# Projecting the raw residual and applying the norm's root to the output, at three stage borders of a two-model float32 kernel

## What is computed

```python
def rms_norm(x, g):
    xf = x.astype(jnp.float32)
    y = xf * lax.rsqrt(jnp.mean(xf * xf, axis=-1, keepdims=True) + EPS)
    return (y * g.astype(jnp.float32)).astype(x.dtype)
...
        u = rms_norm(h, norm_mix_pre[l])
        proj = u @ w_in[l]
...
        x = x + hybrid_mixer(rmsnorm(x, norm_mix_w[l]), w_in[l], ...)
...
        x = x + peer_ffn(rmsnorm(x, norm_ffn_w[l]), peer_wq[l], peer_subkeys[l], peer_u[l], peer_v[l])
```

## Time and profile before

| | |
|---|---|
| median of 3 runs | 3730.04 us (3728.85 to 3734.47) |
| the profiled execution | 3730.55 us |
| its span | 3728.6 us |
| granted TensorE clock, mean | 0.986 of full |
| TensorE busy | 3596.4 us, 96% |
| VectorE, ScalarE, POOL busy | 60%, 40%, 24% |

### The profile page before, as it was taken

One profiled execution on the slowest core, in us unless ns is written; L12 is line 12 of the kernel. 1 busy time (PEld: TensorE's weight loads), 2 busy tenths in 40 slices (PEclk: granted clock), 3 DMA queues, 4 the chain that ended last, 5 costly groups with the idle time before them and its releaser, 6 DMA issues. The chain is left out here.

```text
span 3728.6 us, 55967 instructions
## 1 busy us (share of the span) xinstructions
PE 3596.4 (96%) x22612; PEld 3269.1 (88%) x22612; DVE 2221.1 (60%) x3849; ACT 1477.3 (40%) x2195; POOL 908.5 (24%) x756
## 2 busy tenths in 40 slices
PE   7999999998999999999899998999999999999998
PEld 7988999998887688888577875799999999999998
DVE  5445465554454546555566443269997886777675
ACT  6254453223635435222465433243333333333333
POOL 1010022111101013111114000048966663111110
PEclk9999999999999999999899999999999999999999
DMA  4211232222221133222121221247769999999894
GB/s 145 72 44 62 75 118 97 91 91 68 80 71 55 59 110 109 96 96 92 57 90 52 70 95 57 91 134 244 259 210 263 283 279 336 321 304 310 307 310 141
DMA packets 293615, 544.69 MB, mean 146 GB/s; under 512 B 138288, under 2 KB 187568, under 8 KB 292976
## 3 DMA queue, kind: packets, MB, share of 16 engines
q1 hardware_dynamic: 185248, 394.34, 32.2%
q0 software_dynamic: 27648, 100.68, 8.1%
q10 hardware_dynamic: 80464, 46.10, 4.2%
HBM read 483.67 MB, written 56.62 MB: 145 GB/s over the span
## 5 line engine op out<-in xcount | busy, mean ns | idle before, releaser
L307 PE MATMUL PSM<-UX,PARTS 128*128 128x264 f32 (+3 forms) x3392 | 1164.9, 343 | 55.7 <-DVE UX L336 26.4
L308 PE MATMUL PSM<-UX,PARTS 128*128 128x264 f32 (+3 forms) x3392 | 1147.7, 338 | 0.0
L309 PE MATMUL PSM<-UX,PARTS 128*128 128x264 f32 (+3 forms) x3392 | 1145.7, 338 | 0.0
L265 ACT ACTIVATE PARTS<-RAW 128x1024 fp32r<-128x1024 f32 x612 | 645.4, 1057 | 955.0 <-PE PSM L309 482.5
L275 DVE TENSOR_TENSOR PARTS<-RAW,PARTS 128x1024 fp32r<-128x1024 f32 x549 | 686.0, 1256 | 526.2 <-ACT PARTS L265 520.6
L307 PEld LDWEIGHTS PSM<-UX,PARTS 128*128 128x128 f32 x3392 | 642.7, 189 | 132.6 <-DVE UX L336 36.9
L308 PEld LDWEIGHTS PSM<-UX,PARTS 128*128 128x128 f32 x3392 | 643.2, 190 | 44.2 <-issue 1.7
L309 PEld LDWEIGHTS PSM<-UX,PARTS 128*128 128x128 f32 x3392 | 642.0, 189 | 45.2
L2930 PE MATMUL PSM<-AC,PARTS 128*128 128x416 f32 x1024 | 359.9, 351 | 1.8 <-DVE AC L3214 1.8
L2931 PE MATMUL PSM<-AC,PARTS 128*128 128x416 f32 x1024 | 359.1, 351 | 0.0
L2932 PE MATMUL PSM<-AC,PARTS 128*128 128x416 f32 x1024 | 359.1, 351 | 0.0
(11 more groups left out here) (481 smaller groups left out, 5360.8 us busy)
## 6 DMA issues: line engine op xcount, KB each, us to landing
RAW<-w_ff_dram SPq DMA_DIRECT2D x128, 512.0 KB
RAW<-peer_u_dram SPq DMA_DIRECT2D x128, 512.0 KB
RAW<-peer_v_dram SPq DMA_DIRECT2D x128, 512.0 KB
RAW<-w_in_dram SPq DMA_DIRECT2D x116, 512.0 KB
acts_dram<-MQ ACTq DMA_DIRECT2D x128, 208.0 KB
MQ<-acts_dram SPq DMA_DIRECT2D x128, 208.0 KB
MQ<-gates_dram SPq DMA_DIRECT2D x128, 208.0 KB
RAW<-w_mix_o_dram SPq DMA_DIRECT2D x32, 512.0 KB
```

The costliest lines, as they stand in the source:

```text
L265: e.activation(p[:, 0:1024], self.raw.of(i), ACT.Copy).then_inc(S.sem, S.tick("w", i))
L307: e.matmul(dst, wh[k], xh_[k][:, lo:hi], start=(k == 0), stop=False, skip_group_check=True)
L308: e.matmul(dst, wh[k], xl_[k][:, lo:hi], start=False, stop=False, skip_group_check=True)
L309: m = e.matmul(dst, wl[k], xh_[k][:, lo:hi], start=False, stop=(k == kk - 1), skip_group_check=True)
```

## The change

The residual times the norm's weight, without the root, is split in halves (`raw_rounded` on ScalarE, `raw_rest` on VectorE) as soon as a part of the residual is final, and the first tiles behind each border are made from these raw halves. The root is computed meanwhile and multiplied into the tile where it leaves PSUM, or, for the rotated tiles, into the cosine and sine tables. At the two borders behind a feed-forward the first four tiles run side by side (`four_raw`): for each part of the residual three matmuls into each of four banks; they take two of the four places, and the sum of squares over channels stands between part 5 and part 6. Raw are tiles 0 to 7 of projection 1, the four cx and the four gt tiles of the mixer, and all 16 query tiles. The normed u is still made, for the tiles behind: in projection 1 in pairs of parts during tiles 2 to 5 (`U_AT`), in the mixer in groups during the four gt tiles (`MX_U`), in the queries during tiles 2 to 10. POOL adds the squares, and the last square goes to TensorE by itself. In the mixer the eight-column product moves behind the gt tiles, and VectorE instead of ScalarE takes cx and gt out of PSUM. Two more weight tiles are halved before the feed-forward's last root.

```diff
+        U_AT = {2: (0, 1), 3: (2, 3), 4: (4, 5), 5: (6, 7)}
...
+                if l == 1 and r < 4:
+                    if r == 0:
+                        four_raw(e, 0, [("rot", l, c) for c in range(4)], lo, (("pre", l), TT, sq3[0], ut))
+                    continue
+                xs = ([x[:, lo:] for x in xhs[0]], [x[:, lo:] for x in xls[0]]) if l == 1 and r < 8 else us(lo, TT - lo)
+                tile_pe(e, ("rot", l, r), i0 + r, W.both(i0 + r), xs, TT - lo,
+                        ready=first_ready if r == 8 * l else None)
...
-                ps.give(S, "rot", l, r)
+                if l == 0 or r >= 4:
+                    ps.give(S, "rot", l, r)
+                elif r % 2:
+                    ps.give(S, "rot", l, r - 1)
+                if l == 1 and r in U_AT:
+                    halves_act(e, ("pre", l), ut, TT, ks=U_AT[r])
...
+                e.wait_ge(S.sem, S.at("rstd", ("pre", l)))
+                for x, y in ((cosS, con["cosR"]), (sinS, con["sinR"])):
+                    e.tensor_tensor(x, y, rsX, MUL).then_inc(V.sem, V.tick("tables"))
...
             for r in range(12):
                 sin(r)
+                if l == 1 and r in U_AT:
+                    halves_dve(e, ("pre", l), hT, lambda k: vec(4 * l, k), rsX, ut, TT,
+                               ks=range(U_AT[r][0], U_AT[r][-1] + 3 if r == max(U_AT) else U_AT[r][-1] + 1))
...
+        def raw_rounded(e, l, k):
+            e.wait_ge(V.sem, V.at("h2", l, k))
+            e.activation(xhs[l][k], hT[k][:, 16 * l:], ACT.Copy, scale=next_w(l, k)).then_inc(S.sem, S.tick("xh", l, k))
+
+        def raw_rest(e, l, k):
+            e.wait_ge(S.sem, S.at("xh", l, k))
+            e.scalar_tensor_tensor(out=xls[l][k], in0=hT[k][:, 16 * l:], scalar=next_w(l, k), in1=xhs[l][k].bitcast(F),
+                                   op0=MUL, op1=SUB).then_inc(V.sem, V.tick("xl", l, k))
...
+            def three(c, k):
+                (wh, wl), dst = W.both(i0 + c), PSM[:, slots[c], 0:512]
+                xh_, xl_ = xhs[l][k][:, lo:lo + 512], xls[l][k][:, lo:lo + 512]
+                e.matmul(dst, wh[k], xh_, start=(k == 0), stop=False, skip_group_check=True)
+                e.matmul(dst, wh[k], xl_, start=False, stop=False, skip_group_check=True)
+                m = e.matmul(dst, wl[k], xh_, start=False, stop=(k == 7), skip_group_check=True)
...
+            for k in range(6):
+                e.wait_ge(V.sem, V.at("xl", l, k))
+                for c in range(4):
+                    three(c, k)
+            raw_total(e, *total)
+            for c in range(4):
+                for k in (6, 7):
+                    if c == 0:
+                        e.wait_ge(V.sem, V.at("xl", l, k))
+                    three(c, k)
...
-            e.wait_ge(G.sem, G.at("acc", ("ffpost", l), 7))
-            gemm(e, b, [con["ones"]], [tm[4]], n).then_inc(T.sem, T.tick("ss", ("ffpost", l)))
+            e.wait_ge(G.sem, G.at("acc", ("ffpost", l), 6))
+            e.wait_ge(S.sem, S.at("sq", ("ffpost", l), 7))
+            gemm(e, b, [con["ones"]] * 2, [tm[4], sqf[0]], n).then_inc(T.sem, T.tick("ss", ("ffpost", l)))
...
+                if k == 5:
+                    W.act(e, after_ff(l) + 2)
+            W.act(e, after_ff(l) + 3)
...
+                if k:
+                    raw_rest(e, l, k - 1)
+            raw_rest(e, l, 7)
...
+        MX_U = ((0, 1, 2), (3, 4), (5, 6), (7,))
...
+            four_raw(e, 1, [("cx", o) for o in range(4)], 0, ("mx", T2, sqN[0], utN))
             for o in range(4):
-                tile("cx", o, 0)
+                tile("gt", o, 4)
...
+                e.wait_ge(V.sem, V.at("ul", "mx", kk))
...
             for o in range(4):
-                copy(o)
+                W.act(e, i0 + 4 + o + 3)
+                halves_act(e, "mx", utN, T2, ks=MX_U[o])
+                e.wait_ge(V.sem, V.at("gt", o))
+                e.activation(gt[o], gt[o], ACT.Gelu_apprx_tanh).then_inc(S.sem, S.tick("gt", o))
...
+            def scaled_gt(o):
+                W.dve(e, i0 + 4 + o + 3)
+                halves_dve(e, "mx", xT, lambda k: v2(k), rsN, utN, T2, ks=range(MX_U[o][0], MX_U[o][-1] + (3 if o == 3 else 1)))
+                e.wait_ge(T.sem, T.at("gt", o))
+                e.tensor_tensor(gt[o], PSM[:, ps.of("gt", o), 0:T2], rsN, MUL).then_inc(V.sem, V.tick("gt", o))
+                ps.give(V, "gt", o)
...
+            for o in range(3):
+                scaled_x(o)
+            conv(0)
+            scaled_x(3)
+            e.wait_ge(S.sem, S.at("wab"))
+            e.tensor_tensor(wabs[1], wab, wabs[0].bitcast(F), SUB).then_inc(V.sem, V.tick("wab"))
             for o in range(4):
+                scaled_gt(o)
+            for o in range(1, 5):
                 conv(o)
...
-            W.act(e, first["xo"] + 7 + 3)
+            for o in range(8):
+                W.act(e, first["xo"] + o + 3)
+                e.wait_ge(V.sem, V.at("xo", o))
+                e.activation(xuh[o], xT[o], ACT.Copy, scale=v2(24 + o)).then_inc(S.sem, S.tick("xuh", o))
+                if o >= 3:
+                    e.wait_ge(G.sem, G.at("acc", "pq", o - 2))
+                e.activation(sqP[o], xT[o], ACT.Square).then_inc(S.sem, S.tick("sq", "pq", o))
...
-            norm_pe(e, "pq", T2, Y[0:3])
             for o in range(16):
-                tile_pe(e, ("pq", o), iP + o, W.both(iP + o), us(0, T2), T2, ready=u_ready(e, "pq") if o == 0 else None)
-
+                tile_pe(e, ("pq", o), iP + o, W.both(iP + o), (xuh, xul), T2,
+                        ready=(lambda k: e.wait_ge(V.sem, V.at("xul", k))) if o == 0 else None)
```

More of the change, by code:

```diff
@@ L112, in program @@
                 pass
+            with (nc.sbuf_tensor("HD2", [128, 16 * TT], F),
+                  nc.sbuf_tensor("XL", [128, 8 * TT], FR) as XL):
+                pass
         with (nc.sbuf_tensor("AB", [128, 128], FR) as AB,
@@ L315, in us, with halves_act @@
             return [u[:, lo:lo + n] for u in uh], [u[:, lo:lo + n] for u in ul]
-        def halves_act(e, tag, tmps, n, between=lambda k: None):
-            for k in range(8):
+        def halves_act(e, tag, tmps, n, between=lambda k: None, ks=range(8)):
+            for k in ks:
                 between(k)
@@ new lines, in four_raw @@
+        def four_raw(e, l, events, lo, total):
+            i0 = after_ff(l)
+            slots = []
+            for c in (0, 2):
+                b, back = ps.take(*events[c])
+                seen["ps", events[c + 1]] = (b + 1, ps.i, 0)
+                slots += [b, b + 1]
+                for q, v in back:
+                    e.wait_ge(q.sem, v)
+                for i in (i0 + c, i0 + c + 1):
+                    e.wait_ge(V.sem, V.at("w", i))
+            def three(c, k):
[4 more added lines that the diff above has]
+                m = e.matmul(dst, wl[k], xh_, start=False, stop=(k == 7), skip_group_check=True)
+                if k == 7:
+                    m.then_inc(T.sem, T.tick(*events[c]))
+                    W.parts.give(T, i0 + c)
+            for k in range(6):
[8 more added lines that the diff above has]
+                    three(c, k)
@@ L1734, in mxp_pe @@
             m.then_inc(T.sem, T.tick("ab"))
-            for o in range(1, 4):
-                tile("gt", o, 4)
-            tile("cq", 0, 8)
             tile("cq", 1, 8)
@@ L1748, in mxp_pe @@
                      skip_group_check=True).then_inc(T.sem, T.tick("gc"))
-            tile("cq", 2, 8)
-            lru(2)
-            lru(3)
-            for o in range(3, 9):
+            for o in range(4, 9):
                 tile("cq", o, 8)
@@ L1833, in mxp_act @@
             ps.give(S, "ab")
-            for o in range(4):
-                W.act(e, i0 + 4 + o + 3)
-                e.wait_ge(T.sem, T.at("gt", o))
-                e.activation(gt[o], PSM[:, ps.of("gt", o), 0:T2], ACT.Gelu_apprx_tanh).then_inc(S.sem, S.tick("gt", o))
-                ps.give(S, "gt", o)
-            copy(4)
             e.preload_act_table(ACT.Ln)
```

191 lines of the change are left out of this document (140 added, 51 removed).

## The result

The changed kernel takes **3692.66 us** (median of 4 runs, 3690.94 to 3695.72), before measured beside it 3731.01; the ratio is 0.9897, with a 95% interval of 0.988 to 0.9914. The profiled execution took 3693.49 us, its span is 3691.7 for 3728.6: 36.9 us less, where the forecast had 30.9.

The account below looks back on a forecast made before the run. TensorE, busy 96% of the span, bounds the kernel, losing time at three seams. Gains 19.0 + 9.5 + 2.4 = 30.9 us took the profiled 3730.55 to 3699.6; with the median half a microsecond lower, 3699, range 3688 to 3712.

Parts of the forecast that it names:

- Third seam: Attention output to expert queries: 20.0 us lost, less 0.9 for one sum, gives a gain of 19.0, between 17 and 20.
- Second seam's start: Feed-forward 1 to mixer: first low part at 1806.5, four tiles and total end at 1833.0, 15.9 us ahead.
- residual step: VectorE's work per residual part at the second seam: 1.52 us, made 2.2 by one more pass of 0.75.
- it is not waited for again: Second seam: after the first low part TensorE, 2.8 us per part, never waits for VectorE, 2.2 us per part.
- half clock: TensorE's restart at the second seam: 4.4 us of work at half the granted clock, costing 2.2 us.
- Second seam's rounds: Making normed u in the mixer: 6.6 us per round against TensorE's 5.56; seam's gain 9.5, between 5 and 15.
- First seam: Feed-forward 0 to projection 1: 16.6 us ahead, 14 lost in four rounds of 8.65; gain 2.4, between -3 and 8.
- Tile 6's wait: Projection 1: TensorE stands from 956.6 to 962.4 until tile 3's swaps give back tile 6's banks.
- The lead was not kept in full: Rival, all seams: rounds overlap better, the seams give 16.6, 15.9 and 19, so 51.5 and 3679 us; 10%.
- Rounds dearer by 1 us: Rival, first and second seams: each round costs 1 us more, restarts 2 more each; gain 20, 3710 us; 20%.
- The queries' halves did help: Rival, third seam: early halves don't help as an operand comes late; term falls to 2 or so, 3717 us; 3%.
- The clock came back: Rival, side-by-side tiles: bank changes keep the clock at 0.50; 45 us of half-clocked work per seam gives 3739 us; 3%.

Follow-up runs that it names:

- early: lag's order, with projection 1's pairs of u made in tiles 1 to 4 instead of 2 to 5; 3683.99 us.
- q_only: The kernel before with only the third seam changed, both feed-forward seams left as before; 3706.98 us, ratio 0.9935.
- seq: The whole change, but the four first tiles behind each feed-forward run one after another instead of side by side; 3701.95 us, ratio 0.9926.
- noadds: The whole change without POOL's adds of squares at the first two seams, so the roots hold two of eight squares; 3689.35 us.
- both: The whole change with the changes of lag and align together; 3684.05 us.
- align: The whole change with halves of u and hidden rows laid 512 words apart instead of 528, from layer 1's second mixer-output onwards; 3686.09 us.
- best: The whole change with the changes of early and hdl together; 3678.08 us.
- hdl: align's spacing, and feed-forward 1's high and low hidden halves in separate blocks 4096 words apart; 3691.95 us in one run.
- lag: The whole change, but in projection 1 ScalarE rounds each pair of parts of u one tile after VectorE made it; 3691.47 us.

## Why the prediction was right

3699 us was forecast, 3688 to 3712 the range; 3692.7 came. Step by step:

- **Third seam, 19.0, measured 21.0.** No wait, one sum of 1.02 for 0.9, and no half-clocked start: 19.3 at the second tile. The other 1.7 are fourteen tiles at 5.44 us for 5.56, which no row of before could tell. The mechanism was right, the 1.7 luck.
- **Second seam's start.** Forecast with today's times: first raw tile 1806.5, four tiles ended 1833.0. Measured, with 4.7 added: 1805.95 and 1833.2. Right in sum, and wrong in a step: "Its residual step costs 1.52 per part", with "one more pass of 0.75" to make 2.2. It was 3.2, more than TensorE's 2.8, so that "it is not waited for again" was wrong too, though by little: some 0.2 before part 5 and 0.84 before the sum. It cost no more because TensorE worked its first 3.7 us at half clock and reached VectorE's pace late. Those 3.7 us cost 1.8, for which 2.2 were set down, and the first low part came 0.55 early; that the terms cancel is luck.
- **Second seam's rounds, 9.5, measured 12.1.** The term that was mis-sized is the round (6.6, measured 6.1): the wait in the product was 2.1 for 4.1, the clock did not fall in it (2.2 had been set down for that), and "ends the product at 1867.0" became 1863.5. 1.7 of it went later.
- **First seam, 2.4, measured 3.4.** Swaps forecast to end at 946.2, 950.4, 954.5, 962.4, 971.0, 979.7; they ended at 947.1, 951.2, 955.4, 962.9, 971.2, 979.6. The four tiles ended 1.0 us later than forecast (the slow residual step, which set the time of the sum), and rounds of 7.5 to 8.4 for 8.65 made it good. Tile 6's wait was 5.25 for 5.8, tile 8's 2.25. The mechanism is confirmed by early, which gets 7.3 us back by breaking that chain.
- **Between the seams,** 1.4 us that the forecast had not, and that belong to no part of it (q_only); behind the queries -0.9, whose cause isn't shown.
- **The rivals.** The lead was not kept in full, and early shows why it could be kept further. Rounds dearer by 1 us: they were cheaper by 0.3 and 0.5. The queries' halves did help. The clock came back after 6.0 and 3.7 us of work behind the two gaps (4.4 were set down) and then stood at 1.00 through the side-by-side stretch.

Thus the 6 us by which the forecast was short are 2.6 in the second seam's rounds, 2.0 in the queries, 1.0 in the first seam, 1.4 of chance, less 0.9. The mechanism held at all three seams; that the number lay so near owes something to two errors that cancelled (the residual step against the half clock and the rounds).

## What to carry to other kernels

Norm roots that stand between two projections can leave the path: project the raw halves and scale the output; where nothing else waits for the root the whole gap comes back (19.3 of 20.0). Where another operand still needs the root, follow it to the first tile that uses it, for the lead survives only as far as the engines that make it are ahead; seq gave up 13.7 us of head start for 2.2. Make such an operand in pieces that no engine waits for within a round, and start them early enough that the last piece isn't behind other work. And don't put an add of POOL beside a pacing pass of VectorE that reads two tensors.

## What the runs showed of the hardware

VectorE's passes over two tensors in SBUF stand still for a POOL add that started first: 0.71 us became 1.74, whether tensor_tensor or scalar_tensor_tensor, ending 0.55 to 0.57 behind the add whether that began 0.14 or 1 us before. POOL's pass stands likewise behind VectorE's (1.95 for 1.04).

A 512-column matmul takes 226.7 ns when its moving halves lie 512 words apart and 231.7 on average when they lie 528 apart (up tiles, cq tiles, output tiles, queries, in the same pattern of 225 to 239 each time). The gt tiles, with high halves 512 and low halves 528 words apart, take 233.4. For tiles whose weights are read in halves of 256 columns it stays at 234. The cause is not shown.

The last stage's matmuls (416 columns) come either 190, 184, 191, 189 ns apart, 188.4 on average, or 187 each, in executions of the same stage code, by chance as far as is known: from 3200 on `noadds` and `both` had the even pace, the eleven other traces the uneven one. From 3300 to 3400, the whole change and then `both` (columns as above):

```profile
3300.00:3400.00 100.00, 100.00 (x533) 99.39 (x532) 71.03 (x85) 33.48 (x46) 17.14 (x19) 1.00 0.91 307
```

```profile
3300.00:3400.00 100.00, 100.00 (x537) 100.00 (x537) 71.44 (x85) 34.00 (x46) 17.67 (x19) 1.00 0.90 307
```

Over the 940 us of the stage that is up to 9 us. The even spacing in align may thus only allow the even pace: the 416-column tiles on u had it for a time in align, `both` and best (186.7), and not in hdl (188.4), laid out alike.

The same wait of 2.5 to 3.0 us near 1470 left the clock half-granted for 6.8 us in the kernel before and in `both`, for 3.4 in the whole change and six more, and not at all in `lag`, `seq` and `best`: 1.7 us of the time for each 3.4, by chance. The wait of 2.1 us in the product brought it down in `noadds`, `lag` and `both`; in the seven other traces that have it, the whole change among them, it did not.
